# Three casts put ahead of a root, nine idle products and a reset of the bank turn in a two-block transformer kernel

## What is computed

```python
h = h + 0.5 * rmsnorm(swiglu(rmsnorm(h, n[0]), ffn1_wi[l], ffn1_wo[l]), n[1])
h = h + rmsnorm(hybrid_mixer(rmsnorm(h, n[2]), ...), n[3])
h = h + 0.5 * rmsnorm(swiglu(rmsnorm(h, n[4]), ffn2_wi[l], ffn2_wo[l]), n[5])

def swiglu(x, wi, wo):
    a, b = jnp.split(x @ wi, 2, axis=-1)
    return (jax.nn.silu(a) * b) @ wo
# hybrid_mixer
merged = gates[:, :, 0] * y_f + gates[:, :, 1] * y_sc + gates[:, :, 2] * y_dn
return merged @ w_out
```

## Time and profile before

| | us |
|---|---|
| median of 3 runs | 2758.17 |
| lowest and highest | 2757.0, 2758.91 |
| profiled execution | 2753.36 |
| its span, first to last instruction | 2752.0 |
| TensorE busy | 2632.0 (96%) |
| VectorE busy | 1288.1 (47%) |
| ScalarE busy | 888.8 (32%) |
| mean granted TensorE clock | 0.989 |

### The profile page before, as it was taken

How to read it: one execution, slowest core, us unless ns; L and a number is a source line. 1 busy time by engine, 2 the same in 40 slices (tenths; PEclk the granted TensorE clock), 3 DMA queues, 4 the chain that set the end, 5 groups by cost and what they waited for, 6 DMA issues and landing times.

```text
span 2752.0 us, 38590 instructions
## 1 busy us (share of the span) xinstructions
PE 2632.0 (96%) x16264; PEld 2069.1 (75%) x16264; DVE 1288.1 (47%) x2277; ACT 888.8 (32%) x1320; POOL 148.9 (5%) x201
## 2 busy tenths in 40 slices
PE   8999999999999989999999999999999999899997
PEld 6778787778744333359999999888979776688885
DVE  4446566534423333355343465454444433644444
ACT  4334445333221111133222242444435322431322
POOL 0000000000100000000000000132140400000000
PEclk9999999999999999999999999999999999999998
DMA  4012111134599999963222222211111122223221
GB/s 142 16 63 67 57 58 62 58 138 137 208 412 420 421 420 420 420 279 110 86 93 93 78 83 76 96 51 58 51 58 51 61 90 93 92 92 98 93 88 58
DMA packets 78203, 381.62 MB, mean 139 GB/s; under 512 B 9944, under 2 KB 10200, under 8 KB 52816
## 3 DMA queue, kind: packets, MB, share of 16 engines
q1 hardware_dynamic: 71856, 357.14, 35.3%
q0 software_dynamic: 5456, 20.11, 1.9%
q10 hardware_dynamic: 720, 1.90, 0.2%
HBM read 372.67 MB, written 10.62 MB: 139 GB/s over the span
## 4 chain that ended last, share of the span: by engine, by line
PE 74%; DMA 8%; DVE 4%; ACT 2%; SPq 2%; issue 1%; DVEq 0%; POOLq 0%; ACTq 0%
PE ps L208 72%; DMA rmore<-in_w_ein 5%; DMA ring<-in_w_ein 2%; SPq L293 2%; PE ps L212 1%; ACT L218 1%; DVE ringr L581 0%; DMA vrow<-uT 0%; PE ps L1958 0%; DMA ring<-in_w_hg 0%; DVE uT L472 0%; DVE hT L2660 0%; ACT ringr L575 0%; DMA xg<-vrow,idx 0%; ACT hdd L1227 0%
## 5 line engine op out<-in xcount | busy, mean ns | idle before, releaser
L208 PE MATMUL ps<-uh,ringr 128*128 128x264 f32 (+1 forms) x2256 | 552.7, 340 | 7.2 <-DVE mgb L3946 5.1
L208 PEld LDWEIGHTS ps<-uh,ringr 128*128 128x128 f32 x2256 | 366.2, 189 | 50.9 <-issue 8.6
L208 PE MATMUL ps<-buh,ringr 128*128 128x512 f32 (+1 forms) x1312 | 347.0, 351 | 10.0 <-ACT hg L1209 8.9
L208 PE MATMUL ps<-uTr,ringr 128*128 128x512 f32 (+1 forms) x1136 | 351.3, 346 | 0.0
L581 DVE TENSOR_TENSOR ringr<-ring,ringr 128x1024 fp32r<-128x1024 f32 (+1 forms) x215 | 258.2, 1212 | 141.8 <-ACT ringr L575 141.5
L208 PEld LDWEIGHTS ps<-buh,ringr 128*128 128x128 f32 x1312 | 218.7, 189 | 41.1 <-issue 13.0
L575 ACT CAST ringr<-ring 128x1024 fp32r<-128x1024 f32 (+1 forms) x215 | 219.3, 1036 | 87.2 <-DMA ring<-in_w_fi 33.5
L208 PEld LDWEIGHTS ps<-uTr,ringr 128*128 128x128 f32 x1136 | 197.7, 189 | 22.8 <-issue 3.1
L208 PE MATMUL ps<-ful,ringr 128*128 128x264 f32 (+1 forms) x648 | 169.6, 322 | 0.2 <-DVE ful L508 0.2
L2621 DVE TENSOR_TENSOR fsg<-ps,fsg 128x528 f32<-128x528 f32 (+1 forms) x44 | 30.8, 700 | 198.5 <-PE ps L208 195.1
L208 PE MATMUL ps<-fhh,ringr 128*128 128x264 f32 (+1 forms) x576 | 123.6, 321 | 0.0
(11 more groups left out here) (485 smaller groups left out, 4557.9 us busy)
## 6 DMA issues: line engine op xcount, KB each, us to landing
rmore<-in_w_ein SPq DMA_DIRECT2D x51, 1024.0 KB, 27.0
eahead<-in_w_ein SPq DMA_DIRECT2D x47, 1024.0 KB, 26.7
ring<-in_w_ein SPq DMA_DIRECT2D x30, 1024.0 KB, 27.0
rmore<-in_w_eout SPq DMA_DIRECT2D x27, 1024.0 KB, 27.0
ring<-in_w_fi SPq DMA_DIRECT2D x54, 512.0 KB, 3.7
ring<-in_w_eout SPq DMA_DIRECT2D x19, 1024.0 KB, 27.3
eahead<-in_w_eout SPq DMA_DIRECT2D x18, 1024.0 KB, 27.1
fmore<-in_w_fi SPq DMA_DIRECT2D x34, 512.0 KB, 3.8
```

The source lines that it names most:

```text
L208: return self.P.matmul(out, lhsT, rhs, start=start, stop=stop, skip_group_check=True)
```

## The change

Three edits. In `Ffn.act`, which both feed-forwards use, the call of `ahead_act(0, 5)` is replaced by three casts by name, of parts 4, 5 and 6, ahead of the root. Through `ahead_dve` their low halves move on VectorE as well, ahead of the first product's reading. In `ConvFourier.pe` nine idle products into bank 7 are queued at the start of column two (j = 1). In `MixerEnd.pe` the turn is set to 2 ahead of the eight output products, so that the first one takes banks 4 and 5, and the following ones 0, 2, 4 and so on.

```diff
@@ Ffn.act
-        W.ahead_act(0, 5)
+        for i in range(4, 7):
+            W.cast_act(i)
         self.norm.root_act()
@@ ConvFourier.pe
         for j in range(4):
+            if j == 1:
+                k.busy(7, 9)
             for x in (3, 0, 1, 2) if j else (2,):
@@ MixerEnd.pe
         k.busy(banks[0], 9)
+        k.turn = 2
         for m in range(8):
             w = self.W.halves_pe(m)
```

## The result

| | us |
|---|---|
| median of 4 runs after | 2734.12 (2731.92 to 2735.09) |
| median of 4 runs before | 2757.59 (2755.94 to 2758.91) |
| ratio | 0.9914, 95% interval 0.9897 to 0.9931 |
| profiled execution after, its span | 2735.09, 2733.8 |

The kernel became 23.5 us faster, 0.86%. The forecast was 17.9 us and 2740.3, with a range that ended at 2737.3.

The account below looks back on a forecast made before the run. TensorE, busy 96% of the span, bounds the kernel; only its idle and low-clock time can be won. 10.7 + 2.0 + 3.1 + 2.1 = 17.9 us off 2752.0 gave span 2734.1, median 2740.3 us, range 2737.3 to 2745.6.

Parts of the forecast that it names:

- I take it to be low from 2299 on: Mixer's output: TensorE's clock low for about 3.8 us from the sixth tile, taking back 1.9 of 4.1 us; gain 2.1.
- the four terms: Gains forecast by place: second feed-forward 10.7, first feed-forward 2.0, Fourier stage 3.1, mixer's output 2.1 us; sum 17.9.
- So 2.0 us is all: First feed-forward: only the 2.00 us gap is gained, since the stretch behind it runs at full clock.
- rival (a): Fourier stage: the clock falls all the same despite the idle products; 2743.4 us, chance 0.10.
- lower bound 0: Fourier stage: no gain if the clock falls all the same; the upper bound was 3.1 us.
- rival (c): Mixer's output: the clock stays up through the pieces; 2738.3 us, chance 0.09.
- the pieces' load of 36%: Mixer's output: TensorE works some 0.70 of every 1.93 us ahead of 2299, taken as too little to hold the clock.
- the counter-example: DeltaNet steps, 2249 to 2261: cut by short waits, 10.14 of 12.00 us busy, yet clock 1.00, against the skill's rule.
- (b): Mixer's output: pieces let the clock fall into the second product, paying back all 4.1 us; 2742.4 us, chance 0.09.
- (d): Second feed-forward: part eight late, taking back half of 10.7 us; 2745.7 us, chance 0.04 shared with another case.
- (e): First feed-forward: casts wait for weights and hold the root on ScalarE; 2760.7 us, slower than before, chance 0.01.

## Why the prediction was wrong

**Which step failed.** First the last one of the sum. I took the kernel before at 2758.17, the median of three runs, saw that its profiled execution was 4.8 us lower, and carried this difference over to the changed kernel: 2735.5 became 2740.3. The difference was no property of the kernel. In 61 runs the kernel before has a median of 2755.26, and its comparisons gave 2757.59, 2753.23, 2755.99 and 2755.28, while the changed kernel gave 2734.12, 2734.23 and 2733.97. The three runs shown agreed within 2 us and lay in the upper part of what the kernel does. Of the 6.2 us between 2740.3 and 2734.12, 2.9 are this base (2758.17 less 2755.26). The range took in what I did not know of the edits, and nothing for the base they are subtracted from. Set on 2755.26 it would be 2734.4 to 2742.7, which still leaves 2734.12 just outside. The other failed steps are in the terms: the clock's price at the mixer, put at 1.9 us ("I take it to be low from 2299 on") where it was none, and that in the first feed-forward, put at none where the mean is 1.1. The Fourier stage's and the second feed-forward's were put too high, so that the four terms together are only 0.4 us too small. What is left of the 6.2 us, 2.9, is not explained.

**Second feed-forward: right in waiting, a little large by the clock.** The gap went from 7.76 us to none, the root and VectorE were on time as worked out, and the clock's share was seen by itself. 10.7 us is inside the interval of the single edit (8 to 17). With the mean of five draws it is 7.8 plus 2.3, 10.1. That term was 0.6 too large.

**First feed-forward: right in waiting, too small by the clock.** "So 2.0 us is all" was read from one execution in which the clock held. Of six traces with this gap it held in two (the kernel before and 29 idle products at the mixer) and fell in four, as in the rows of the turn alone:

```profile
1252.23 0.81 PE L208 MATMUL ps<-uh,fmore1r 128*128 128x264 f32 x2 [1.98 <-DVE fmore1r L581]
...
1252.23:1256.23 4.00, 4.00 (x20) 4.00 (x21) 3.72 (x5) 0.68 (x2) 0.00 (x0) 0.57 0.18 71
```

Each time it costs about 1.7 us, so the mean price of the gap is 2.0 plus 1.7 by 4/6, 3.1 us. That term was 1.1 too small.

**Fourier stage: right mechanism, too large.** The gap of 2.69 us cost 3.07 us in the trace I had. Of seven traces with it the clock fell in four and stayed at 1.00 in three; two more stretches behind the same gap:

```profile
1660.01:1664.01 4.00, 4.00 (x22) 4.00 (x23) 3.96 (x6) 0.64 (x2) 0.00 (x0) 0.62 0.00 0
```

```profile
1653.53:1657.53 4.00, 4.00 (x32) 4.00 (x33) 3.97 (x6) 0.64 (x1) 0.00 (x0) 1.00 0.00 0
```

By half the time at 0.50 the four cost 3.1, 1.5, 1.4 and 1.5 us; the mean over seven is 1.1. The single edit measured 0.3. So rival (a) was the wrong question: with the idle products the clock holds, but without them it often holds as well. I gave as lower bound 0 for the wrong reason and took the upper one as the value. This term was 2.0 too large.

**Mixer's output: too small.** 2.1 forecast, 3.9 by the pair of traces, 4.0 by the mean, 4.4 by the single edit; it is rival (c), with a chance of 0.09. The step that failed is "I take it to be low from 2299 on": the clock was 1.00. I weighed the pieces' load of 36%, which by the view's measure is 49%, and not the idle products that stand in front of the first product. The Trainium skill's rule on short idle times between groups (TensorE: Matmul & The Clock Gate, "A second HAM failure mode: psum-queue depth-cycling") is borne out by the kernel without these products, clock 0.51, and not by the changed one, 1.00. Nor is DeltaNet the counter-example that the prediction took it for: its steps ran at 1.00 in all fourteen traces, but behind the gap of 1.00 us that follows them the clock fell in six of fourteen. The mixer's term was 1.9 too small.

**The clock behind each gap.** All fourteen traces together (the cost at the mixer is the distance from low halves to copy less the 5.30 us at full clock, elsewhere half the time at 0.50):

| place | gap, us | traces with it | clock fell in | cost of a fall, us |
|---|---|---|---|---|
| end of DeltaNet, not touched | 1.00 | 14 | 6 | 1.7 |
| first feed-forward | 2.0 | 6 | 4 | 1.7 |
| Fourier stage | 2.69 | 7 | 4 | 1.4 to 3.1 |
| mixer's output | 5.09 | 6 | 6 | 1.4 to 2.8 |
| second feed-forward | 7.76 | 5 | 5 | 1.8 to 3.0 |

**The sum again.** 10.1, 3.1, 1.1 and 4.0 make 18.3 us. The forecast's 17.9 is near it by luck: its four terms are off by -0.6, 1.1, -2.0 and 1.9 (measured less forecast). The timed runs say more: 19.0 (14 to 22) and 21.3 us (17 to 25) in the two later comparisons of the changed kernel, 23.5 (19 to 28) in the first, and 21.0 between the medians of all runs (2755.26 less 2734.23). The step from 18.3 to 21.0 is not settled. It is less than the stretch ahead of the first edit varies between executions, and the median of all runs mixes comparisons in which the kernel before differs by itself: 2753.23 in 21 runs on one chip, 2755.99 in 19 on another, further apart than their scatter explains. The fifth place where the clock falls, at the end of DeltaNet, is in code that both kernels have, and no run shows that the change makes a fall there less frequent.

**The direction and the rivals.** Faster was right; so was that the change does at all four places what it says. (b), (d) and (e) did not come. The table of stretches was read too narrowly: besides the three there is a fourth one at 0.50 in the second half, the last 16.9 us, in which TensorE is busy for 2.0; the change doesn't touch it. The distance of ScalarE's last cast to the root in the first feed-forward, 1.29 us here and forecast at about 1, is a thin margin; VectorE's low halves in the second have one of 1.1.

## What to carry to other kernels

- Ahead of a stage's serial tail (a root, a table load), look at what is queued behind it that needs nothing of it. Here three casts moved from behind the root to ahead of it took away 7.8 us of waiting and 2 to 3 us of clock.
- A gap that sometimes brings the clock down must be priced over several executions. One trace tells of the wait, not of the clock's share of it; a gap of 2 us cost 2.0 us in one trace and 3.7 in another.
- Before a forecast in microseconds is set on a median of few runs, its spread belongs in the range. Three runs within 2 us were 3 us beside the median of 61. And compare within one chip: the medians of one kernel on two chips were 2.8 us apart.

## What the runs showed of the hardware that I had not expected

- The same gap of 2.0 us ahead of the same code was followed by clock 1.00 in two executions and by a mean of 0.57 to 0.59 over 4 us in four. The one of 2.69 us was followed by 1.00 in three and by low clock for 2.9 to 6.1 us in four. At the end of DeltaNet a gap of 1.00 us was followed by full clock in eight and by low clock for 3.4 us in six. Outcomes differ where the code ahead is the same, up to the gap, so it is not that code which decides it.
- Groups of three matmuls in every 1.93 us (busy 1.88 of 3.80 us) kept the full clock for 4.5 us in the six traces in which nine idle products stood in front of the first product, and lost it in the one in which they did not (0.51 over 5.7 us).
- Idle products cost TensorE nothing that shows where it waits. With the wait left as it was, the clock behind was 1.00 with 29 and with 31 of them, one trace each; where these two gaps were left open it fell in all eleven traces, at a cost of 1.4 to 3.0 us.
